# Six more gate tiles projected inside the gated tiles, Silu and Sigmoid applied late, and the long convolution's rounds ordered by filter with the next forward pair ahead of an inverse

## What is computed

```python
def hyena_mixer(h, ...):
    u = short_conv(p[..., :3 * 1024], conv_w, conv_b)
    parts = jnp.split(u, 3, axis=-1)
    z = parts[0]
    for o in range(2):                       # two filters
        z = parts[o + 1] * long_conv(z, k_f[:, o], skip[o])
    return (z * jax.nn.silu(gate)) @ w_out

def second_block(x, ...):
    proj = rmsnorm(x, norm_mix_w) @ w_in     # all projections of the four mixers, and 4 x 1024 gates
    ya = hgrn2_branch(...)   # 4 heads: gated linear attention, rmsnorm(o) * silu(hg)
    yb = ssd_branch(...)
    yc = gla_branch(...)     # 4 heads in 2 tiles: the same, rmsnorm(o) * silu(gg)
    yd = rglru_branch(...)
    gates = jax.nn.sigmoid(mg)
    merged = jnp.sum(gates * branch_out, axis=2)
```

## Time and profile before

| what | us |
|---|---|
| median of 3 runs | 5220.36 (5216.55 to 5220.53) |
| the profiled execution | 5216.07 |
| its span in the profile | 5214.3 |
| TensorE busy | 4836.2 |
| VectorE busy | 1997.6 |
| ScalarE busy | 988.1 |

### The profile page before, as it was taken

One profiled execution on the slowest core, in us unless ns is written; L12 is line 12 of the kernel. 1 busy time (PEld: TensorE's weight loads), 2 busy tenths in 40 slices (PEclk: granted clock), 3 DMA queues, 4 the chain that ended last, 5 costly groups with the idle time before them and its releaser, 6 DMA issues.

```text
span 5214.3 us, 40015 instructions
## 1 busy us (share of the span) xinstructions
PE 4836.2 (93%) x16966; PEld 2373.9 (46%) x16966; DVE 1997.6 (38%) x2340; ACT 988.1 (19%) x1318; POOL 3.9 (0%) x7
## 2 busy tenths in 40 slices
PE   7989999996999988889888898999999999999998
PEld 3446565542444434344455444444444444444443
DVE  3445555313333366563454544423511124333102
ACT  1134444202111100001333232222200000000000
POOL 0000000000000000000000000000000000000000
PEclk8999999997999999999999999999999999999999
DMA  5100000112232322222000001112221111111211
GB/s 234 60 29 1 1 1 1 45 39 110 89 105 94 140 89 111 93 113 74 33 21 22 25 33 41 37 41 77 83 89 39 36 63 49 41 46 43 72 40 51
DMA packets 85693, 313.95 MB, mean 60 GB/s; under 512 B 9061, under 2 KB 27237, under 8 KB 77450
## 3 DMA queue, kind: packets, MB, share of 16 engines
q1 hardware_dynamic: 68156, 293.57, 15.6%
q10 hardware_dynamic: 17360, 17.83, 1.0%
HBM read 254.22 MB, written 57.15 MB: 60 GB/s over the span
## 4 chain that ended last, share of the span: by engine, by line
PE 64%; DVE 9%; issue 2%; ACT 2%; DMA 0%; DVEq 0%; SPq 0%; ACTq 0%
PE late_dense L115 40%; PE late_four L2787 6%; PE late_two L2787 3%; PE late_four L1023 3%; PE late_four L1241 1%; PE late_four L2022 1%; PE late_two L1320 1%; PE late_two L1312 1%; PE late_four L1040 1%; PE late_four L1035 1%; DVE late_arena L2232 1%; PE late_two L1258 1%; PE late_two L2345 0%; PE late_two L2347 0%; PE late_two L2048 0%
## 5 line engine op out<-in xcount | busy, mean ns | idle before, releaser
L115 PE MATMUL late_dense<-late_arena 128*128 128x512 f32 x5416 | 2378.8, 599 | 24.7 <-DVE late_arena L2705 10.0
L115 PEld LDWEIGHTS late_dense<-late_arena 128*128 128x128 f32 x5416 | 1035.1, 192 | 1313.5 <-issue 1301.8
L128 ACT ACTIVATE late_arena<-late_dense 128x512 f32<-128x512 f32 x226 | 134.8, 597 | 1396.3 <-PE late_dense L115 1383.3
L2787 PE MATMUL late_four<-late_arena 128*128 128x512 f32 x752 | 326.6, 592 | 0.0
L115 PE MATMUL attn_dense<-attn_h,attn_wbuf 128*128 128x512 f32 x576 | 253.3, 598 | 7.6 <-DVE attn_h L551 6.6
L2787 PEld LDWEIGHTS late_four<-late_arena 128*128 128x128 f32 x752 | 142.9, 190 | 179.8 <-issue 176.7
L659 PE MATMUL attn_dense<-matrices,attn_work 128*128 128x128 f32 x1280 | 193.9, 282 | 32.0 <-ACT attn_work L707 15.8
L2705 DVE TENSOR_TENSOR late_arena<-late_dense,late_arena 128x512 f32<-128x512 f32 x64 | 44.2, 691 | 420.1 <-PE late_dense L115 420.1
L2022 PE MATMUL late_four<-late_arena 128*128 128x128 f32 (+1 forms) x1024 | 119.4, 318 | 84.9 <-DVE late_arena L2165 54.5
L1023 PE MATMUL late_four<-late_arena 128*128 128x512 f32 x384 | 171.5, 600 | 9.7 <-DVE late_arena L1057 6.6
L659 PEld LDWEIGHTS attn_dense<-matrices,attn_work 128*128 128x128 f32 x1280 | 135.2, 140 | 92.5 <-issue 58.8
(11 more groups left out here) (374 smaller groups left out, 4889.2 us busy)
## 6 DMA issues: line engine op xcount, KB each, us to landing
attn_q<-in_ada_w SPq DMA_DIRECT2D x12, 2048.0 KB, 9.5
late_arena<-in_w_ffn_in SPq DMA_DIRECT2D x44, 512.0 KB, 4.2
late_arena<-in_hy_tables SPq DMA_DIRECT2D x16, 1280.0 KB, 6.1
late_arena<-in_hy_w_in SPq DMA_DIRECT2D x32, 512.0 KB, 3.5
spectrum<-late_arena SPq DMA_DIRECT2D x8, 2048.0 KB, 8.5
late_arena<-spectrum SPq DMA_DIRECT2D x8, 2048.0 KB, 12.5
late_arena<-in_w_gates SPq DMA_DIRECT2D x32, 512.0 KB, 3.4
late_arena<-x SPq DMA_DIRECT2D x6, 2048.0 KB, 10.2
```

The costliest lines, as they stand in the source:

```text
L115: mm = pe.matmul(self.ps[:, n % SEG], self.wbuf[:, slot, k], job.rhs[:, k, cols], start=(job.first and k == 0), stop=(job.last and k == kt ...
L128: act.activation(job.out[:, cols], self.ps[:, n % SEG], job.func, scale=job.scale, bias=job.bias).then_inc(self.emptied[n % SEG], 1)
L2787: mm = pe.matmul(product_bank(M, name, i), left[:, k], right[:, k], start=(k == 0), stop=(k == 3))
```

## The change

It has four parts. `SPILLED` goes from 12 to 18: gates 0 to 5 are projected in tiles 0 to 2, two in each, and the gates that were 0 to 4 in tiles 4 and 5 become 6 to 10, those behind the z rows 11 to 17. `fills` gets 12 segments instead of 8 for tiles 0 to 2, one after each level 1 to 6, and spreads the 14 of tiles 3 and 5 in the same way. Spilled gates and the `hg` and `gg` rows are evicted by plain copies; Silu is applied to the row behind the norm's Sqrt, and Sigmoid to the row that was brought back. The convolution's rounds become (0,0), (0,1), (1,0), (1,1), both halves of the input are loaded ahead of round 0, and each next round's first pair is issued ahead of the inverse.

```diff
+ROUNDS = ((0, 0), (0, 1), (1, 0), (1, 1))
...
     sp.dma_start(Y.z[0], A["turned"][0].rearrange("q p (h c) -> h p q c", h=2)[0]).then_inc(Y.z_in, 16)
-    order = [(0, 0), (1, 0), (0, 1), (1, 1)]
+    sp.dma_start(Y.z[1], A["turned"][0].rearrange("q p (h c) -> h p q c", h=2)[1]).then_inc(Y.z_in, 16)
...
-        if j == 1:
-            sp.dma_start(Y.z[1], A["turned"][0].rearrange("q p (h c) -> h p q c", h=2)[1]).then_inc(Y.z_in, 16)
...
-    for j, (o, half) in enumerate(((0, 0), (1, 0), (0, 1), (1, 1))):
+
+    def first_pair(j):
+        o, half = ROUNDS[j]
         s, n, z = 2 * STEPS + 2 * j, 2 * STEPS + 4 * j, Y.z[half]
         if o == 0:
-            pe.wait_ge(Y.z_in, 16 * (half + 1))
+            pe.wait_ge(Y.z_in, 32)
         else:
-            pe.wait_ge(Y.inv_read, 8 * j)
+            pe.wait_ge(Y.inv_read, 8 * (half + 1))
         pe.wait_ge(Y.group_read, n) if j else pe.wait_ge(Y.x_ready, s)
         pair_pe(pe, Y, s, 0, z, z)
+
+    first_pair(0)
+    for j, (o, half) in enumerate(ROUNDS):
...
         dense.multiply(pe, 3)
+        if j + 1 < len(ROUNDS):
+            first_pair(j + 1)
         pe.wait_ge(Y.back_in, 16)
...
-SPILLED = 12
+SPILLED = 18
...
         def gate(n, after=None):
-            into_ring(f"gate{n}", A["w_gates"][n], ACT.Sigmoid, after)
+            into_ring(f"gate{n}", A["w_gates"][n], ACT.Copy if n < SPILLED else ACT.Sigmoid, after)
...
-            into_ring(f"hg{h - 1}", w["hg"][h - 1], ACT.Silu)
+            gate(2 * h - 2)
+            gate(2 * h - 1)
+            into_ring(f"hg{h - 1}", w["hg"][h - 1], ACT.Copy)
...
-        return {"v": 1, 1: 1, 3: 1, 5: 1, 7: 2, "k": 1, "u": 1, "o": 0}
-    if g == 3:
-        return {"v": 2, 1: 2, 2: 2, 3: 2, 4: 2, 7: 2, "k": 1, "u": 1, "o": 0}
-    if g == 4:
-        return {"v": 2, 1: 1, 2: 1, 3: 1, 4: 1, 5: 1, 6: 1, 7: 3, "k": 1, "u": 1, "o": 1}
-    return {"v": 2, 1: 1, 2: 1, 3: 1, 4: 1, 5: 0, 6: 1, 7: 3, "k": 1, "u": 2, "o": 1}
+        return {"v": 1, 1: 1, 2: 1, 3: 1, 4: 1, 5: 1, 6: 1, 7: 2, "k": 1, "u": 1, "o": 1}
+    return {"v": 2, 1: 1, 2: 1, 3: 1, 4: 1, 5: 1, 6: 1, 7: 3, "k": 1, "u": 1, "o": 1}
...
+    for name in M.tiles[g].names:
+        M.dense.done(act, name)
+        act.activation(M.ring_row(name), M.ring_row(name), ACT.Silu).then_inc(M.gate_silued, 1)
...
-            M.dense.done(dve, name)
+            dve.wait_ge(M.gate_silued, n + 1)
...
+        else:
+            use = M.ring_use[f"back{n}"]
+            row = M.ring_row(f"back{n}")
+            act.wait_ge(M.ring_in[use % 3], 16 * (n // 3 + 1))
+            act.activation(row, row, ACT.Sigmoid).then_inc(M.opened, 1)
...
         if n < SPILLED:
-            dve.wait_ge(M.ring_in[use % 3], 16 * (n // 3 + 1))
+            dve.wait_ge(M.opened, n + 1)
```

More of the change, by code:

```diff
@@ L1122, in hyena_sp @@
     sp.dma_start(Y.z[0], A["turned"][0].rearrange("q p (h c) -> h p q c", h=2)[0]).then_inc(Y.z_in, 16)
-    order = [(0, 0), (1, 0), (0, 1), (1, 1)]
+    sp.dma_start(Y.z[1], A["turned"][0].rearrange("q p (h c) -> h p q c", h=2)[1]).then_inc(Y.z_in, 16)
     at = 4 * STEPS + 1
-    for j, (o, half) in enumerate(order):
+    for j, (o, half) in enumerate(ROUNDS):
         for f in range(2):
@@ L1175, in load_last @@
 def load_last(sp, Y, half, tiles):
-    j = 2 * half + 1
+    j = 2 + half
     for c in tiles:
@@ L1279, in hyena_pe @@
     turn_pe(pe, Y, 14)
-    for j, (o, half) in enumerate(((0, 0), (1, 0), (0, 1), (1, 1))):
+    def first_pair(j):
+        o, half = ROUNDS[j]
         s, n, z = 2 * STEPS + 2 * j, 2 * STEPS + 4 * j, Y.z[half]
         if o == 0:
-            pe.wait_ge(Y.z_in, 16 * (half + 1))
+            pe.wait_ge(Y.z_in, 32)
         else:
-            pe.wait_ge(Y.inv_read, 8 * j)
+            pe.wait_ge(Y.inv_read, 8 * (half + 1))
         pe.wait_ge(Y.group_read, n) if j else pe.wait_ge(Y.x_ready, s)
         pair_pe(pe, Y, s, 0, z, z)
+    first_pair(0)
+    for j, (o, half) in enumerate(ROUNDS):
+        s, n, z = 2 * STEPS + 2 * j, 2 * STEPS + 4 * j, Y.z[half]
         dense.multiply(pe, 1)
@@ L1627, in evict_dve @@
         if o == 0:
-            loads = half * (2 + (2 if q % 4 < 2 else 0)) + q // 4 + 1
+            loads = 2 * half + q // 4 + 1
             dve.wait_ge(Y.factor_in[q % 4], 16 * loads)
@@ L1632, in evict_dve @@
             c, pair = divmod(q, 2)
-            loads = 2 + half * 4 + c // 2 + 1
+            loads = 4 + 2 * half + c // 2 + 1
             dve.wait_ge(Y.factor_in[c % 2], 16 * loads)
@@ L1751, in __init__ @@
         self.lru_rate_act, self.lru_rate_dve = (ph.sem(s) for s in ("lru_rate_act", "lru_rate_dve"))
-        self.masks_in = ph.sem("masks_in")
+        self.masks_in, self.opened, self.gate_silued = (ph.sem(s) for s in ("masks_in", "opened", "gate_silued"))
         self.freed = [ph.sem(f"freed{s}") for s in range(3)]
@@ L1812, in __init__ @@
         add("gv1", w["gv"][1], xn, tiles[4].raws[1], after=(self.ab_filled, use["v", 3, 0] + 1))
-        into_ring("hg3", w["hg"][3], ACT.Silu)
+        into_ring("hg3", w["hg"][3], ACT.Copy)
         add("gf1", A["gla_gate_w"][:, 1:2], low, tiles[5].f, ACT.Identity, bias=small[:, 5:6],
@@ L1819, in __init__ @@
         add("gv3", w["gv"][3], xn, tiles[5].raws[1], after=(self.ab_filled, use["v", 4, 1] + 1))
-        gate(0)
-        gate(1)
-        into_ring("gg0", w["gg"][0], ACT.Silu)
-        into_ring("gg1", w["gg"][1], ACT.Silu)
-        for n in range(2, 5):
+        gate(6)
+        gate(7)
+        into_ring("gg0", w["gg"][0], ACT.Copy)
+        into_ring("gg1", w["gg"][1], ACT.Copy)
+        for n in range(8, 11):
             gate(n)
-        into_ring("gg2", w["gg"][2], ACT.Silu)
-        into_ring("gg3", w["gg"][3], ACT.Silu)
+        into_ring("gg2", w["gg"][2], ACT.Copy)
+        into_ring("gg3", w["gg"][3], ACT.Copy)
         for t in (4, 5, 0, 1, 2, 3):
@@ L1834, in __init__ @@
             into_ring(f"z{t}", w["sz"][t], ACT.Silu)
-        for n in range(5, SPILLED):
+        for n in range(11, SPILLED):
             gate(n)
@@ L1854, in __init__ @@
                     needs=[(self.hidden_made, 2 * (FT - PLAIN))] if m == 0 else ())
-        self.spills = [f"gate{n}" for n in range(5)]
+        self.spills = [f"gate{n}" for n in range(11)]
         self.spills += [f"{kind}{t}" for t in range(4) for kind in ("lx", "lg")]
-        self.spills += [f"gate{n}" for n in range(5, SPILLED)]
+        self.spills += [f"gate{n}" for n in range(11, SPILLED)]
     def next_inputs(self, h, w):
@@ L2691, in merge_dve @@
         name = f"back{n}" if n < SPILLED else f"gate{n}"
-        gate, use = M.ring_row(name), M.ring_use[name]
+        gate = M.ring_row(name)
         if n < SPILLED:
-            dve.wait_ge(M.ring_in[use % 3], 16 * (n // 3 + 1))
+            dve.wait_ge(M.opened, n + 1)
         else:
```

## The result

The changed kernel takes 5134.51 us (median of four runs, 5130.36 to 5136.31), against 5220.44 for the kernel before on the same chip: a ratio of 0.9835, 95% interval 0.9818 to 0.9852. The forecast was 5136. The profiled execution took 5130.36 us, with a span of 5128.6, which is 85.7 us less than before; the sum had said 82.6.

What follows compares the result with a forecast made beforehand. TensorE, busy 93% of the span, was taken as the bound. Rounds -22.2 us, and tiles +22.2 with merge -82.6 giving -60.4, sum to -82.6; from starting points giving 5133.5 and 5137.8 it said 5136, range 5120 to 5158.

Steps and rivals of the forecast that it cites:

- Forecast A: Whole kernel: both parts work as costed, -82.6 us to 5136, own range 5122 to 5150; chance 0.70.
- what could eat it: Convolution rounds' gain of 22.2 us: the early pair waits for the next table, or VectorE must first read the banks.
- rival C: Convolution: rounds get no shorter, because the chain is VectorE's or the table comes late; 5158 us, chance 0.06.
- The second half's transfer: Before round 0: the input's second half lands at no cost, 1.2 us to spare; bound 2.4 us.
- Rival D: Tiles 1 and 2: gaps at levels 5 and 7 stay, 14.7 us in each tile; 5165 us, chance 0.10.
- Rival E: Tiles 0 to 3: each product waits for the segment just ahead, 122 us in all; 5258 us, chance 0.03.
- just fit: Level 5 of the gated tiles: VectorE's factors end 10.5 us after segment 3, against 10.4 us of TensorE work.
- Rival B: Tiles 1 to 5: ScalarE must empty before switching to Silu, 1.06 us each; 5141 us, chance 0.09.
- near 5.5: Tile 4: wait before level 7, where Silu makes the 3.16 us wait 2.35 longer.
- so they hide nothing and the wait of 10.64 stays in kind: Tile 3: segments at levels 5 and 6, 0.86 us each, leave level 7's wait; the tile's term is -4.9 us.
- the term of -5.2: Tile 5: segment of 6.88 moved into waits, level 7 pushed back 3.0, level 0 gives 1.3; -5.2 us.
- Rival F: Merge: returned rows come late without cover, up to 5.6 us and a Sigmoid each, 40 us; 5176, chance 0.02.

Runs made afterwards that it cites:

- Experiment 1: The convolution's part of the change alone (rounds, their loads and counts), on the kernel before: 5194.67 us, ratio 0.9954.
- Experiment 3: Changed kernel with rounds still by filter, but each first pair of matmuls back behind the inverse: 5153.79 us, ratio 0.9876.
- experiment 7: Changed kernel with idle copies ahead of the late Silu, one in tile 0's norm and three in tile 1's: 5137.10 us, one execution.
- Experiment 5: Changed kernel with the ten output gates' Silu back in their evictions, Sigmoid still late, segments at new places: 5133.19 us, ratio 0.9837.
- experiment 2: The part on the gated tiles alone (six more gate tiles, late Silu and Sigmoid), on the kernel before: 5154.52 us, ratio 0.9876.
- experiment 8: Changed kernel with one segment multiplied ahead of level 7's product in tiles 3 to 5, evicted where it was: 5111.35 us, ratio 0.9796.
- experiment 4: Kernel before with only Silu and Sigmoid taken out of the evictions and done late, old segment places: 5213.80 us, ratio 0.9992.
- experiment 6: Changed kernel with every Silu and Sigmoid back in its eviction, segments and 18 returned rows at new places: 5135.78 us, ratio 0.9842.
- experiment 9: Changed kernel with one more segment ahead of three inverses and VectorE's early-pair sums between two evictions: 5118.03 us, ratio 0.9811.

## Why the prediction was right, and where it was off

**The rounds.** Forecast A held. Waits of 6.55 before three inverses and 13.43 before the last, and none behind an inverse, are those named. Experiments 1 and 3 show that the pair's place carries it. The extra 1.7 us are luck: the restarts I kept whole differ from round to round (the inverses took 30.70, 30.84, 30.31 and 30.64 us before, and 30.71, 30.33, 29.51 and 30.63 after), and by their starts the four were 1.7 us shorter. What I named under "what could eat it", the table, did come late, in round 1 (2.04 us, and 8.80 for the pair), but the pair behind it then waited 1.86 less for VectorE, and another pair of 8.83 us became one of 7.13. Experiment 1, this part alone with 24.7 us, rules out rival C.

**The second half's transfer.** It landed 16.7 us after 1810.5, at 1827.2, and the first pair started at 1827.46 without a wait. I had said 1.2 us to spare; it was 0.3. The mechanism was right, the size too kind.

**Tiles 0 to 2.** 112.5, 107.2 and 107.3 us, where I said "near 113" and 107.7. Tiles 1 and 2 wait 1.33 at level 1 and under 0.2 at every other level; tile 0 keeps its 6.01. The comparison with tile 4's layout in the earlier trace rows was the reading that made this safe. Rivals D and E are gone with it. Level 5 was said to "just fit", 10.5 against 10.4 us: in the trace VectorE's second factor ends at 2647.31 and the product starts at 2647.36, 0.05 us later than the segment ahead of it would allow. So the two were level, and experiment 7 shows that each pass more is waited for.

**Rival B and its rule.** Timeline of ScalarE in tile 1, around the norm (answers to the earlier trace rows):

```profile
2640.12 1.06 ACT L2127 ACTIVATE late_arena<-late_arena 128x1024 f32<-128x1024 f32 x1 [1.08 <-DVE late_arena L2237]
2641.19 1.28 ACT L2130 ACT_TABLE_LOAD   x1
2642.49 1.06 ACT L2130 ACTIVATE late_arena<-late_arena 128x1024 f32<-128x1024 f32 x1
2643.56 1.28 ACT L2081 ACT_TABLE_LOAD   x1
2644.86 1.06 ACT L2081 ACTIVATE late_arena<-late_arena 128x1024 f32<-128x1024 f32 x1
```

Sqrt, load, Silu, load and exponential follow each other within 0.02 us; the added switch and Silu cost 2.37 us (2643.56 - 2641.19), as taken from the rows. The Trainium skill, "ScalarE: Activation LUTs", section "What ACT_TABLE_LOAD costs", adds a drain of some 1.38 us to every switch. This trace does not agree: nothing stands between the ACTIVATE and the load.

**Tile 4.** I had put the Silu's 2.35 us on level 7. It showed at level 5 instead, 1.85 us, and level 7 rose only from 3.16 to 3.60, with a slow block of 3.78. The two together are 5.45, the "near 5.5" of the forecast: the size was right, and the place was not. The total, +3.6, is in the range I gave (1 to 4). Experiment 5, with Silu early, has 3.16 at level 7 and none at level 5 again, which shows the cause.

**Tiles 3 and 5.** The step that failed is "so they hide nothing and the wait of 10.64 stays in kind". The wait before level 7 of tile 3 fell to 8.15, with one of 1.89 ahead of it where 1.25 was: 1.85 us less for the two, about what two segments of 0.86 can hide. The term of -4.9 measured -5.9.

In tile 5 the term of -5.2 measured -8.3. Timeline of TensorE, the product behind level 0's wait and the second norm sum, before and then after:

```profile
3095.00 3.79 PE L2022 MATMUL late_four<-late_arena 64*128 64x128 f32 x32 [5.28 <-DVE late_arena L2179]
...
3128.00 1.98 PE L2061 MATMUL late_two<-late_arena,matrices 128*128 128x512 f32 x4 [1.32 <-DVE late_arena L2229]
```

```profile
3097.55 2.06 PE L2027 MATMUL late_four<-late_arena 64*128 64x128 f32 x32 [3.86 <-DVE late_arena L2187]
...
3127.80 1.98 PE L2066 MATMUL late_two<-late_arena,matrices 128*128 128x512 f32 x4 [1.32 <-DVE late_arena L2237]
```

From the tile's start (3070.66 and 3074.32) to the product behind level 0's wait it is 24.34 us before and 23.23 after (-1.1, said: -1.3). From there to that norm sum it is 33.00 and 30.25: the block and the segment behind the wait did not run slowly this time, and 2.75 us are gone that the sum did not have. From the norm sum to the product of level 7 (3169.77 and 3172.50) it is 41.77 and 44.70, +2.9 for the Silus (said: +3.0). It shows in a new wait of 2.80 at level 5 and one of 12.70 at level 7, together 15.5, where I had "near 15" at level 7 alone. From there to the end it is 85.08 and 77.68: the segment of 6.88, and 0.5 of restarts. So the term that failed is the restart behind level 0's wait, put at no change. Why it came off stays open: the equal wait of tile 4 (3.85 us) was followed by a block of 3.79, and behind the same 3.86 in tile 5 the block took 2.06 in experiment 2 too, but 2.57 and 2.73 in experiments 7 and 8. TensorE's busy time fell by more, 5.7 us (143.79 to 138.11), with the same 604 records. The rest of that is mostly the restart behind the old wait of 4.83 us at level 6 (block and segment, 3.79 and 8.33 us). It gave no time, as the wait of 12.70 before level 7 is for VectorE.

**Luck in the sum.** The total is nearer than its terms. Against the forecast, the tiles are 4.7 us better (+17.5 for +22.2, by the rows of the table), the rounds 1.7, and the stretch behind the last norm sum 0.6; the end of the kernel is 2.2 worse, and 1.65 were there before the change begins. Together that is the 3.1 us between 82.6 and 85.7. That the median, 5134.5, came within 1.5 us of the 5136 is closer than either sum or median is known.

**What the sum did not ask.** I costed the late Silu as a part of the mechanism. Experiments 4 to 6 show that the change would be as fast without either late pass. ScalarE's queue had 4.7 us of chain against 8.8 us of matmuls; two loads of 1.28 fit into that.

**The merge.** Twelve segments came off the end in full: from the merge's second product to the start of the last 704 records it is 1152.3 before and 1070.2 after, or 82.1 for 82.6 forecast. The last 704 took 302.37 and then 304.00 us, the same instructions. The longest of the 18 returned rows landed after 14.0 us, not 5.6; ScalarE waited for these rows 15 times, and TensorE never. Rival F's price was too low, its cover of 20.6 us was enough.

## What to carry to other kernels

Work that costs its full length at a saturated end is worth moving into any wait, and the row to look for is one that already stands in the wanted layout: tile 4 told how tiles 0 to 2 would run. A wait that is filled can give back the slow restart behind it as well (TensorE's busy time fell by 19 us here, beside 66 of idle time), so count both, and count the restart only where no other engine's chain sets the time. When a wait has been removed, look at what is issued in what order for the next one: the table behind two filters cost 15 us in experiment 9, until the second filter went behind it.

## What the hardware showed beyond that

The slow restart in numbers, table by stretch of TensorE in the changed kernel, the start of an inverse behind a wait of 6.55 us and the 6.9 us behind that (the last three numbers are granted clock, share of DMA, GB/s):

```profile
1925.70:1932.50 6.80, 6.80 (x9) 2.83 (x10) 1.08 (x2) 0.00 (x0) 0.00 (x0) 0.56 0.19 77
1932.50:1939.40 6.90, 6.90 (x17) 3.04 (x16) 1.42 (x3) 0.00 (x0) 0.00 (x0) 1.00 0.24 76
```

and in experiment 9, where a pair and a segment run up to the inverse:

```profile
1926.30:1953.80 27.50, 27.50 (x66) 12.19 (x65) 7.93 (x10) 0.60 (x1) 0.00 (x0) 1.00 0.16 58
```

Half the clock (1.2 instead of 2.4 GHz) for most of the first stretch, full clock behind it and all through the second case. Which wait is followed by it is not fixed: blocks behind 3.01 and 1.85 us ran at 2.05 and 2.06, the block behind 1.89 us in tile 3 took 3.52, and behind 2.76 us one took 2.05 and the next 3.78 in the same run (experiment 6). In the changed kernel's tiles all blocks behind 3.60 us and more were slow, but for one of 2.06 behind 3.86 in tile 5. In the tiles each cost some 1.5 to 3 us with the segment behind it, so a forecast of single restarts is good to a few us and no better.
